# Late modulation groups of the first up product: weighed and added on VectorE, with four small TensorE products per group

## The reference, cut to what matters

```python
def modulation(cond, w, b):
    return jnp.split(jax.nn.silu(cond) @ w + b, 6, axis=-1)      # w: (1024, 6144), cond: 2 vectors

def conv_ffn(h, w_up, w_conv, w_down):
    u = dwconv(h @ w_up, w_conv)                                 # w_up: (1024, 5632), 3 taps
    val, gate = jnp.split(u, 2, axis=-1)
    return (jax.nn.silu(gate) * val) @ w_down
```

## Time and profile before

| | before |
|---|---|
| median of 3 runs (lowest, highest) | 1529.36 us (1528.19, 1535.52) |
| span of the profiled execution | 1523.4 us |
| TensorE busy | 1414.5 us, 93% |
| VectorE busy | 892.0 us, 59% |
| ScalarE busy | 617.3 us, 41% |
| mean granted TensorE clock | 0.971 |

### The profile page before, as it was taken

The page is one execution under the profiler, slowest core; times in us unless marked ns, Lnnn a source line. Parts: engine busy times, 40 slices in busy tenths (PEclk is TensorE's granted clock), DMA queues, the critical chain, the costliest instruction groups (busy, mean ns, idle before and its releaser), DMA issues. The chain is left out here.

```text
span 1523.4 us, 30761 instructions
## 1 busy us (share of the span) xinstructions
PE 1414.5 (93%) x13475; PEld 1184.6 (78%) x13475; DVE 892.0 (59%) x1307; ACT 617.3 (41%) x1036; POOL 119.6 (8%) x136
## 2 busy tenths in 40 slices
PE   3798999889999999999999999989999999899998
PEld 2566576778887788777778888877887778899998
DVE  3549634445463566655565314688776686788844
ACT  2323544221232244433433214453453794555534
POOL 1000000232233020000000000200001100000000
PEclk8999989899999999999999999999999999999999
DMA  9321101145325131665562233212233004366643
GB/s 329 91 83 55 56 28 37 36 139 168 114 79 144 55 118 59 181 176 166 166 180 97 84 110 118 70 55 84 83 116 128 7 29 142 114 188 180 180 166 111
DMA packets 170255, 172.28 MB, mean 113 GB/s; under 512 B 15270, under 2 KB 135946, under 8 KB 170122
## 3 DMA queue, kind: packets, MB, share of 16 engines
q1 hardware_dynamic: 167728, 165.14, 35.7%
q0 software_dynamic: 1088, 4.19, 0.7%
q10 hardware_dynamic: 1306, 0.99, 0.2%
HBM read 169.26 MB, written 1.05 MB: 112 GB/s over the span
## 5 line engine op out<-in xcount | busy, mean ns | idle before, releaser
L676 PE MATMUL bank<-h,w_hi 128*128 128x256 f32 (+1 forms) x952 | 328.3, 345 | 2.9 <-issue 2.9
L315 DVE TENSOR_TENSOR w_lo<-w_raw,w_hi 128x2048 fp32r<-128x2048 f32 (+1 forms) x91 | 206.9, 2274 | 193.0 <-ACT w_hi L305 192.8
L680 PE MATMUL bank<-h,w_lo 128*128 128x256 f32 (+1 forms) x952 | 319.7, 336 | 0.0
L679 PE MATMUL bank<-h,w_hi 128*128 128x256 f32 (+1 forms) x952 | 319.6, 336 | 0.0
L305 ACT ACTIVATE w_hi<-w_raw 128x2048 fp32r<-128x2048 f32 x93 | 176.5, 1899 | 191.0 <-PE bank L676 141.2
L694 DVE SCALAR_TENSOR_TENSOR acc<-bank,params,acc 128x510 f32<-128x510 f32 (+3 forms) x272 | 173.1, 646 | 90.6 <-ACT acc L1734 64.4
L676 PEld LDWEIGHTS bank<-h,w_hi 128*128 128x128 f32 x952 | 182.1, 191 | 37.1 <-issue 18.7
L679 PEld LDWEIGHTS bank<-h,w_hi 128*128 128x128 f32 x952 | 182.1, 191 | 20.1 <-issue 2.9
L680 PEld LDWEIGHTS bank<-h,w_lo 128*128 128x128 f32 x952 | 181.7, 191 | 18.8
L1734 ACT ACTIVATE acc<-bank,params 128x512 f32<-128x512 f32 (+1 forms) x88 | 48.6, 580 | 155.8 <-PE bank L680 58.4
L676 PE MATMUL bank<-h_hi,w_hi_hyb 128*128 128x512 f32 (+1 forms) x184 | 77.3, 420 | 11.5 <-DVE dn_qkv L694 4.4
(11 more groups left out here) (428 smaller groups left out, 2861.2 us busy)
## 6 DMA issues: line engine op xcount, KB each, us to landing
w_raw<-in_ffn_up SPq DMA_DIRECT2D x86, 512.0 KB, 5.3
w_raw<-in_mod_w SPq DMA_DIRECT2D x40, 1024.0 KB, 5.2
w_raw<-in_ffn_down SPq DMA_DIRECT2D x22, 1024.0 KB, 4.9
w_raw<-in_ssm_w_in SPq DMA_DIRECT2D x20, 1024.0 KB, 5.3
w_raw<-in_hyb_w_in SPq DMA_DIRECT2D x9, 1024.0 KB, 5.3
w_raw<-in_ssm_w_out SPq DMA_DIRECT2D x8, 1024.0 KB, 4.9
mod_early<-in_mod_w SPq DMA_DIRECT2D x4, 1024.0 KB, 17.6
mod_early<-in_mod_w POOLq DMA_DIRECT2D x4, 1024.0 KB, 14.6
```

Of the source, the lines that this page charges most:

```text
L315: dve.tensor_tensor(lo, raw, hi.bitcast(F32), ALU.subtract).then_inc(k.lo_done.sem, 1)
L676: mm = pe.matmul(out, wh, xh, start=(start and n == 0), stop=False)
L679: pe.matmul(out, wh, xl, start=False, stop=False)
L680: mm = pe.matmul(out, wl, xh, start=False, stop=(stop and n == last))
```

## The change

The modulation halves of groups 16 to 23 are no longer multiplied by TensorE. VectorE multiplies each block of 128 rows by the conditioning value of its row and adds the blocks up (`mod_weigh`, eight instructions per group: two behind the taps of each half of a slot, in iterations 2 to 17). TensorE then adds the 128 partitions of the sum with four products of 2 columns against ones (`mod_columns`, in the even slots 4 to 18, after m = 0). `mod_row` and `mod_turn` are left out for this batch. Both result columns now hold the value for the latent tokens' vector `c` (column 15 of `condpad`); the context tokens, which had the other column, are no longer used where layer 1 applies groups 16 to 23 (its mixer's gate and its feed-forward block).

```diff
+MOD_COLUMNS = 16
+def mod_weigh(k, dve, m, part):
+    g, half = divmod(m, 2)
+    load = k.mod_load[m]
+    w = k.stream.raw[:, load % 2, :].rearrange("p (k n) -> p k n", k=4)
+    if part == 0:
+        await_load(k, dve, load)
+    if part == 0 and half == 0 and g - MOD_COLUMNS >= 2:
+        dve.wait_ge(k.mod_turned, mod_batch(g) + g - MOD_COLUMNS - 1)
+    acc = k.modacc[:, g % 2, :]
+    for j in range(2 * part, 2 * part + 2):
+        cond = k.condpad[:, 4 * half + j, 15:16]
+        if half == 0 and j == 0:
+            ins = dve.tensor_scalar(acc, w[:, j, :], cond, None, ALU.mult)
+        else:
+            ins = dve.scalar_tensor_tensor(out=acc, in0=w[:, j, :], scalar=cond, in1=acc, op0=ALU.mult, op1=ALU.add)
+        if j < 3:
+            k.vchain.link(dve, ins)
+        else:
+            ins.then_inc(k.mod_used.sem, 1)
+    if part == 1 and half == 0:
+        dve.wait_ge(k.mod_used.sem, m + 1)
+def mod_columns(k, pe, g):
+    pe.wait_ge(k.mod_used.sem, 2 * g + 2)
+    for j in range(4):
+        c = 8 * (g - MOD_COLUMNS) + 2 * j
+        mm = pe.matmul(k.pb[7][:, c:c + 2], k.modacc[:, g % 2, j * P:j * P + P], k.ones[:, 0:2], start=True, stop=True)
+    mm.then_inc(k.mod_turned, 1)
...
@@ FfnUp.pe
-                if m == 0 and self.mods is not None and 2 <= s < 18:
-                    mod_products(k, pe, self.mods + s - 2)
-            if self.mods is not None and s == 20:
-                mod_turn(k, pe, mod_batch(self.mods // 2))
+                if m == 0 and self.mods is not None and 4 <= s < 20 and s % 2 == 0:
+                    mod_columns(k, pe, (self.mods + s - 4) // 2)
...
@@ FfnUp.act
-            if self.mods is not None and s == 18:
-                mod_row(k, act, mod_batch(self.mods // 2))
...
@@ FfnUp.dve
                 conv_taps(k, dve, acc[:, i % 4, :], self.bank(i), self.taps(i), 3, self.n // LC).then_inc(self.conv_done.sem, 1)
+                if self.mods is not None and 2 <= s < 18:
+                    mod_weigh(k, dve, self.mods + s - 2, m)
```

More of the change, by code:

```diff
@@ L422, in mod_bias @@
     ng = b - a
-    dve.wait_ge(k.mod_turned, n + 1)
+    in_columns = a >= MOD_COLUMNS
+    dve.wait_ge(k.mod_turned, n + (ng if in_columns else 1))
     at = COL[f"mod_b{layer}"] + 4 * i
@@ L426, in mod_bias @@
     mod = k.mod[:, layer, 4 * i:4 * i + 4 * ng, :].rearrange("p (g j) s -> p g j s", j=4)
-    turned = k.pb[7][:, 0:8 * ng].rearrange("p (j g s) -> p g j s", j=4, s=2)
+    turned = k.pb[7][:, 0:8 * ng].rearrange("p (g j s) -> p g j s" if in_columns else "p (j g s) -> p g j s", j=4, s=2)
     dve.tensor_tensor(mod, turned, bias, ALU.add).then_inc(k.mod_out, 1)
@@ L3474, in build_program @@
         b.xn = put("norm_xn", 160, [P, 3, T])
-        k.modrow = put("mod_row", 160, [P, 512])
+        k.modacc = put("mod_products", 160, [P, 2, 512])
         b.xf = put("ssm_x", 160, [P, 4, T])
```

## The result

| | before | after |
|---|---|---|
| median (lowest, highest of the undisturbed runs) | 1530.99 us of 4 (1528.19, 1535.52) | 1671.03 us of 3 (1670.44, 1674.32) |
| span of the profiled execution | 1523.4 us | 1672.5 us |
| ratio after to before | | 1.0912, 95% interval 1.0878 to 1.0947 |

The changed kernel is 9.1% slower, some 140 us. A fourth execution of it took 1766.55 us at a granted clock of 0.778 and is left out as disturbed; the median with it is 1672.67.

The account below looks back on a forecast made before the run. TensorE was taken to bound the kernel before, a closed chain of load, split and VectorE's iteration after. 146.7 + 1.7 - 0.9 = 147.5 us, with 1523.4 and 6.0, gave 1677 us, 9.6% slower; 80% range 1645 to 1702.

Parts of the forecast that it names:

- The ring: Layer 0 up product: late release, load, split and rest of iteration follow one another; 21.37 us per slot against 12.11; 82%.
- load: From issue of a modulation half, up load behind it, to ScalarE's high part: 9.34 us, bounds 8.3 and 9.9.
- weighing: Four VectorE instructions of 128x512 at the end of each of 16 iterations: 2.72 us, 0.68 each.
- The rival in which only the loads are late: Up product slots: VectorE and ScalarE not held, slot 17.4 us, 80 us more over 15 slots, 1609 us; chance 6%.
- The rival in which the low clock sets the pace: TensorE at the lower clock through whole slots, 22 to 23.5 us a slot, about 1700 us; chance 7%.
- The one in which TensorE stays the bound: Up product slots: load and split fit into one slot, 1516 us; chance 3%.
- The multiplication by a scalar alone: One of eight weighing instructions per group, taken at about 0.68 us; the skill's 0.42 would lower the total by 2 us.
- From where to where: From iteration 2's taps at 612.71 to slot 19 ready at 949.1, which before began at 802.4: 146.7 us later.
- The clock: TensorE at the lower clock after idling: hidden in each slot's wait, counted once at slot 19, +1.7 us.
- Signs that came otherwise: Profile after, 620 to 945 us: TensorE idle about 10 us per slot, ScalarE's w_hi waiting about 9 us each.
- The 6.0 us around the span: Time taken to lie around the profiled span against the median, added to 1670.9 to give 1676.9 us.
- The sum that did not apply: If TensorE stayed the bound: -19.7 modulation products, -0.9 mod_turn, +7.2 small products, -13.4 us.

Follow-up runs that it names:

- experiment 7: Kernel before, modulation products still on TensorE, with two extra buffers for the modulation halves: 1532.17 us, ratio 1.0005.
- experiment 5: Changed kernel with one of three products (high weights by low activations) left out in slots 4 to 17: 1665.6 us, ratio 1.0881.
- Experiment 1: Kernel before, with the modulation half given free by a small VectorE instruction at the iteration's end, no weighing or small products: 1625.8 us, ratio 1.0621.
- 2: Changed kernel with all four weighing instructions of an iteration moved directly behind the weight split: 1587.56 us, ratio 1.0386.
- 3: Changed kernel with one block of 128 rows loaded per modulation half instead of four: 1636.63 us, ratio 1.0699.
- 4: Changed kernel with two of four weighing instructions per iteration left out (blocks 1 and 2 of each half not added): 1643.31 us, ratio 1.0726.
- experiment 6: Changed kernel with the modulation halves in two buffers of their own, issued behind the up loads: 1519.07 us, ratio 0.9931.

## Why the prediction was right

It named 1677 us, 147.5 more than before; the measured median is 1671, 140 more. Step by step:

- **What bounds.** Right. TensorE was the bound before. The extra buffers under the old products (experiment 7) show that the loads did not set the pace then, and the third product left out (5) shows that TensorE does not set it now.
- **The ring.** Right in place, order and links. Experiment 1 shows that the late release alone closes it, 2 that its length is what lies between split and release, 3 and 4 that load and weighing are links of it. The rival in which only the loads are late asked for a period of 17.4 us; the changed kernel's is 21.00. The rival in which the low clock sets the pace falls with experiment 5. The one in which TensorE stays the bound falls with the gaps between TensorE's slots.
- **Its length**, 21.37 us forecast, 21.00 measured. The *load* was 9.34 in the sum and is 8.82 on average. The sum stood on one example, and 9.34 lies inside the 8.61 to 9.78 of the 15 loads after; why single loads differ by up to 1.2 us stayed open. The *weighing* was 2.72 and is 3.09 in half of the turns (643.70 to 648.24, less the second pair of taps) and 2.82 in the others. The combined operation takes 750 ns and not 681, so the row on 16 partitions that I went by was the wrong neighbour, and the one with an input from PSUM was the right one. The four *taps* were 2.96 and are 2.90. The errors of load (-0.52) and weighing (+0.24 on average) had opposite signs, so the period came out closer than its terms: that part is luck.
- **The multiplication by a scalar alone** takes 0.48 us where the sum had 0.68. Here the estimate from the Trainium skill ("VectorE: DVE Perf Modes", The perf-mode tier table), 0.42, is the nearer one. Below is the instruction, with the one behind it. The difference of 0.20 us is worth 1.6 us over the eight groups:

```profile
622.94 0.48 DVE L418 TENSOR_SCALAR mod_products<-w_raw,cond_padded 128x512 f32<-128x512 f32 x1
623.46 0.75 DVE L420 SCALAR_TENSOR_TENSOR mod_products<-w_raw,cond_padded,mod_products 128x512 f32<-128x512 f32 x1
```

- **From where to where.** Slot 19 was to begin at 949.1 and began at 952.32. But the whole stretch came late: SP issued up 3 at 601.59 where the earlier trace rows has 592.82, 8.8 us, in a part of the program that the change does not touch. Without it the difference at slot 19 is 952.32 - 802.4 - 8.8 = 141.1 us, against 146.7 forecast; the 0.37 us per turn make 5.5 of that. With the clock and without `mod_turn` that is 141.1 + 1.7 - 0.9 = 141.9 us, where 140.0 lie between the medians.
- **The clock.** Right in size. Slot 19 took 12.6 us from its first product (952.32) to that of slot 20 (964.87) in place of 10.9, 1.7 more. In the ring TensorE stood idle from 628.6 to 640.4 us; the granted clock fell to 0.64 between 630 and 635 and was 0.50, the lower level of 1.2 GHz, from 635 to 645. In the 4 us from the first product of each of the slots 4 to 19 it was 0.50 to 0.63. Inside the ring this did not set the pace (experiment 5). The Trainium skill says in "TensorE: Matmul & The Clock Gate", HAM oscillation, that a wait for a load in each tile makes every next tile start at the lower level. The trace agrees with that, for all 16 slots; the 27 us that the prediction worked out by this rule, and did not add, are not in the measured time.
- **Signs that came otherwise.** ScalarE's high part was to wait about 9 us each time for the up load and waited 14.2. The load accounts for 8.8 of it; ScalarE is also idle from its last seed to the end of VectorE's iteration (642.8 to 648.2 us above), which the sign left out. TensorE was to stand idle about 10 us per slot and stood idle 7.4, since it works more than 2 us longer in each slot at the lower clock. For the same reason the small products, forecast to wait about 2 us in each even slot, waited 0.6 us in all: m = 0 ends about when the iteration does. None of this changes the time.
- **The 6.0 us around the span** were no such thing. The profiled execution after took 1674.32 us with a span of 1672.5, so 1.8 lie around it. It is the same for the kernel before (1531.13 with a span of 1529.3, in a run beside experiment 1). So its profiled execution took 1523.4 + 1.8 = 1525.2 us and was faster than the four in the table above (1528.19 to 1535.52). The difference of 147.5 us went by the rows and is not affected. Span plus 6.0 is nothing but the median, so the sum reached the right place although its reason was wrong.
- **The sum that did not apply**, -13.4 us if TensorE stayed the bound, is near what experiment 6 measured: -11.8 between the medians, and -6.7 to -14.2 by the interval of the ratio.

## What to carry to other kernels

Before moving work to an engine with time to spare, look at what the old place gave free and who waits for that: the release of a buffer moves with the work, and everything behind it in an in-order queue moves too. Write down the chain from the release through the load to the first instruction that needs it, and add up what the engine does from there to the next release; if that is longer than the slot, the engine's idle share says nothing. Take the buffer out of the shared ring first; then move the work.

## What the runs showed of the hardware that was not expected

- Profiled executions reach the same instruction at different times with the same code ahead of it: up 3 was issued at 592.82 (before), 601.59 (after), 596.73, 598.74, 597.08, 600.71 and 594.43 us (experiments 1 to 5). The granted clock between 230 and 590 us, a stage of small products, was 0.97 in the first and 0.94 in the second, and 0.95 or 0.96 in the others, which lie between them; that the clock makes the difference was not tested. A difference of two spans carries these 9 us; the median of the runs and the period within the stage do not.
- Modulation half and up load, 2 MB issued within 1.6 us, could be used 8.6 to 9.8 us after the first issue (15 pairs, most of them under 8.9), and with a quarter of the modulation half the period was 2.1 us shorter.
